# A streaming-encoder block in exact float32 products: narrow columns in the first value block's passes, norm weights on GpSimd's queue

## What is computed

```python
h = rms_norm(x, norm_gain)
proj = einsum('btd,de->bte', h, w_in)              # 9296 columns
qa, ka, va, ga, qb, kb, vb, gb, qi, ki, wi = split(proj)   # 8 x 1024, 1024, 64, 16
out_a = chunked_relpos_attention(qa, ka, va, rel_bias)
logits = einsum('bqhd,bsd->bqhs', qi, ki)
score = einsum('bqh,bqhs->bqs', wi * idx_scale, relu(logits))
sel = top_k(where(admissible, score, -inf), 64)
out_b = attention(qb, kb[sel], vb[sel], alibi)     # 8 heads of 128
y = concat(out_a * silu(ga), out_b * silu(gb))
out = rms_norm(x + y @ w_out, final_gain)
```

## Time and profile before

| | us |
|---|---|
| median of 3 runs | 530.44 (530.16 to 530.63) |
| the profiled execution's own time | 529.62 |
| its span from the first to the last instruction | 527.6 |

### The profile page before, as it was taken

One profiled execution on the slowest core, in us unless ns is written; L12 is line 12 of the kernel. 1 busy time (PEld: TensorE's weight loads), 2 busy tenths in 40 slices (PEclk: granted clock), 3 DMA queues, 4 the chain that ended last, 5 costly groups with the idle time before them and its releaser, 6 DMA issues.

```text
span 527.6 us, 8251 instructions
## 1 busy us (share of the span) xinstructions
PE 519.2 (98%) x2871; PEld 451.9 (86%) x2871; DVE 366.7 (70%) x551; ACT 273.8 (52%) x405; POOL 29.8 (6%) x46
## 2 busy tenths in 40 slices
PE   9999999999999999999999999999999999999994
PEld 6899998888888888888888888888888888888883
DVE  6898685665668766767676767586877887646454
ACT  6875544444543344445554637374655566434342
POOL 1005043150000000000000000000000000000000
PEclk9999999999999999999999999999999999999998
DMA  8966966658555555563746454645555775665614
GB/s 298 381 205 187 288 203 214 196 174 279 172 190 196 197 199 183 182 196 106 234 145 194 148 176 157 191 147 183 159 160 176 252 250 170 189 198 194 202 44 159
DMA packets 72668, 102.53 MB, mean 194 GB/s; under 512 B 3504, under 2 KB 61760, under 8 KB 72384
## 3 DMA queue, kind: packets, MB, share of 16 engines
q1 hardware_dynamic: 70944, 96.68, 56.7%
q0 software_dynamic: 1264, 5.00, 3.0%
q10 hardware_dynamic: 432, 0.47, 0.3%
HBM read 99.24 MB, written 2.11 MB: 192 GB/s over the span
## 4 chain that ended last, share of the span: by engine, by line
PE 98%; DVE 0%; ACT 0%; DVEq 0%; issue 0%
PE acc L426 38%; PE acc L424 18%; PE acc L391 11%; PE acc L392 11%; PE acc L393 11%; PE acc L429 1%; PE aux L496 1%; PE acc L457 1%; PE aux L585 1%; PE aux L606 1%; PE acc L439 1%; PE aux L611 0%; PE aux L583 0%; PE aux L612 0%; PE aux L613 0%; PE aux L527 0%
## 5 line engine op out<-in xcount | busy, mean ns | idle before, releaser
L426 PE MATMUL acc<-acts,w_hi 128*128 128x512 f32 (+1 forms) x896 | 304.8, 389 | 0.0
L960 DVE TENSOR_TENSOR w_lo<-w_raw,w_hi 128x1024 fp32r<-128x1024 f32 x172 | 213.2, 1244 | 107.3 <-ACT w_hi L674 106.0
L674 ACT ACTIVATE w_hi<-w_raw 128x1024 fp32r<-128x1024 f32 x172 | 181.7, 1058 | 156.8 <-PE acc L426 81.9
L424 PE MATMUL acc<-acts,w_lo 128*128 128x256 f32 (+1 forms) x840 | 232.8, 277 | 0.0
L426 PEld LDWEIGHTS acc<-acts,w_hi 128*128 128x128 f32 x896 | 166.5, 188 | 30.1
L424 PEld LDWEIGHTS acc<-acts,w_lo 128*128 128x128 f32 x840 | 158.6, 189 | 1.0
L391 PE MATMUL acc<-w_hi,acts 128*128 128x512 f32 x248 | 96.6, 389 | 0.0
L392 PE MATMUL acc<-w_lo,acts 128*128 128x512 f32 x248 | 96.5, 389 | 0.0
L393 PE MATMUL acc<-w_hi,acts 128*128 128x512 f32 x248 | 96.5, 389 | 0.0
L391 PEld LDWEIGHTS acc<-w_hi,acts 128*128 128x128 f32 x248 | 46.6, 188 | 10.0 <-issue 0.3
L392 PEld LDWEIGHTS acc<-w_lo,acts 128*128 128x128 f32 x248 | 46.6, 188 | 9.6
(11 more groups left out here) (179 smaller groups left out, 388.1 us busy)
## 6 DMA issues: line engine op xcount, KB each, us to landing
w_raw<-w_blocks SPq DMA_DIRECT2D x140, 512.0 KB, 3.6
w_raw<-wo_blocks SPq DMA_DIRECT2D x32, 512.0 KB, 4.3
w_raw<-w_blocks SPq DMA_DIRECT2D x8, 256.0 KB, 5.3
qk<-x POOLq DMA_DIRECT2D x1, 2048.0 KB, 10.7
qk<-xT SPq DMA_DIRECT2D x7, 256.0 KB, 6.0
o<-ext_dram POOLq DMA_DIRECT2D x1, 1024.0 KB, 8.1
fgain<-final_gain POOLq DMA_DIRECT2D x1, 1024.0 KB, 7.8
out<-o SPq DMA_DIRECT2D x2, 512.0 KB, 3.0
```

The costliest lines, as they stand in the source:

```text
L424: nc.tensor.matmul(acc[:, bank:bank + n], w_lo4[:, u % RING, q, c], a_hi[:, k, tokens], start=False, stop=False)
L426: last = nc.tensor.matmul(whole, w_hi4[:, u % RING, q, c], acts[:, k, :, tokens], start=(k == 0), stop=(k == KT - 1))
L674: nc.scalar.activation(flat(w_hi[:, s, :, :]), w_raw[:, s, :], ACT.Copy).then_inc(hi_done, 1)
L960: nc.vector.tensor_tensor(flat(w_lo[:, s, :, :]), w_raw[:, s, :], flat(w_hi[:, s, :, :]).bitcast(f32), ALU.subtract).then_inc(lo_done, 1)
```

## The change

The weights of block 0 get 80 more columns: every k of a slot is now 592 wide (512 of va and 80 narrow), and each of its passes is made as two of 296 columns, the first into the old bank of `acc`, the second into `aux[0]` or `aux[1]` (216 columns of va and the 80 narrow ones, with tokens on partitions). The narrow passes, the copies and the three transposes go. Each unit's narrow weights come by a DMA of their own (two pieces of 320 bytes for each partition). The first k is loaded and split in parts of 296 columns and the rest; its narrow piece is issued on ScalarE's queue in the gain's old place, and the gain is GpSimd's first instruction. The norm sums move from after unit 2 of block 1 to after unit 0, block 0's results are read in two pieces each, the narrow ones straight from `aux`, and the transposes of `ki_nat` move from after unit 7 to before unit 6. The diff, cut:

```diff
+WIDE = CB + NARROW
+PART = WIDE // 2
+V_REST = CB - PART
...
+        raw_slots = sb("raw_slots", [P, RING, UK * WIDE])
...
+            def load_narrow(u):
+                sp.dma_start(raw_slots[:, u % RING, :].rearrange("p (k c) -> p k c", k=UK)[:, :, CB:WIDE],
+                             w_narrow[:, u * UK * NARROW:(u + 1) * UK * NARROW].rearrange("p (k c) -> p k c", k=UK)
+                             ).then_inc(nw_landed[u % RING], 16)
+
             for u in range(HALVED):
-                sp.dma_start(w_raw[:, u, 0:CB], w_blocks[VA_FIRST, u, :, 0:CB]).then_inc(half_landed[u], 16)
                 if u == 0:
+                    sp.dma_start(raw_slots[:, 0, 0:PART], w_blocks[VA_FIRST, 0, :, 0:PART]).then_inc(first_landed, 16)
+                    sp.dma_start(raw_slots[:, 0, PART:CB], w_blocks[VA_FIRST, 0, :, PART:CB]).then_inc(half_landed[0], 16)
                     sp.dma_start(xT_land[:, 1, :], xT[:, 1, :]).then_inc(xT_landed[0], 16)
-                sp.dma_start(w_raw[:, u, CB:2 * CB], w_blocks[VA_FIRST, u, :, CB:2 * CB]).then_inc(w_landed[u], 16)
+                else:
+                    load_narrow(u)
+                    sp.dma_start(raw_slots[:, u, 0:CB], w_blocks[VA_FIRST, u, :, 0:CB]).then_inc(half_landed[u], 16)
+                sp.dma_start(raw_slots[:, u, WIDE:WIDE + CB], w_blocks[VA_FIRST, u, :, CB:2 * CB]
+                             ).then_inc(w_landed[u], 16)
...
-            sp.dma_start(nw_raw[:, :], w_narrow).then_inc(nw_landed, 16)
...
         def _(pool):
+            pool.dma_start(gain[:, :], norm_gain).then_inc(gain_landed, 16)
...
-            pool.wait_ge(narrow_done, 1)
             split_q(0)
...
+            def wide_pass(k, part, a, w, start=False, stop=False):
+
+                c = (k % UK) * WIDE + part * PART
                 for m in range(TM):
-                    nc.tensor.matmul(acc[:, m * CB:m * CB + CB], a[:, 0, m * P:m * P + P], w[:, 0, 0, :],
-                                     start=start, stop=False)
+                    dst = (acc[:, m * CB:m * CB + PART], aux[m][:, 0:PART])[part]
+                    last = nc.tensor.matmul(dst, a[:, k, m * P:m * P + P], w[:, (k // UK) % RING, c:c + PART],
+                                            start=start, stop=stop)
+                return last
 
             pe.wait_ge(a0_done, 1)
+            pe.wait_ge(first_hi, 1)
+            wide_pass(0, 0, a_hi, hi_slots, start=True)
             pe.wait_ge(half_hi, 1)
-            first_k(a_hi, w_hi, True)
+            wide_pass(0, 1, a_hi, hi_slots, start=True)
             pe.wait_ge(alo_done, 1)
-            first_k(a_lo, w_hi, False)
+            for part in range(2):
+                wide_pass(0, part, a_lo, hi_slots)
+            pe.wait_ge(first_lo, 1)
+            wide_pass(0, 0, a_hi, lo_slots)
             pe.wait_ge(half_lo, 1)
-            first_k(a_hi, w_lo, False)
...
+                    for n, (a, w) in enumerate(((a_hi, hi_slots), (a_hi, lo_slots), (a_lo, hi_slots))):
+                        for part in range(2):
+                            last = wide_pass(k, part, a, w, stop=(k == KT - 1 and n == 2))
                 last.then_inc(mm_done, 1)
...
-            for u in range(3):
-                feature_unit(1, u, 1, CHUNK)
+            feature_unit(1, 0, 1, CHUNK)
             pe.wait_ge(cleared, 3 + HEADS)
             pe.wait_ge(summed, UNITS)
             nc.tensor.matmul(aux[2][:, 0:T], ones_mat[:, :], x_sum[:, 0:T], start=True, stop=True)
...
-            feature_unit(1, 3, 1, CHUNK)
-
-            pe.wait_ge(nlo_done, 1)
-            for k in range(KT):
-                for n, (w, a) in enumerate(((nw_hi, a_hi), (nw_hi, a_lo), (nw_lo, a_hi))):
-                    last = nc.tensor.matmul(aux[0][0:NARROW, 0:T], w[:, k, :], a[:, k, :],
-                                            start=(k == 0 and n == 0), stop=(k == KT - 1 and n == 2))
-            last.then_inc(narrow_done, 1)
+            for u in range(1, 4):
+                feature_unit(1, u, 1, CHUNK)
             both_out(1)
...
             act.dma_start(xT_land[:, 0, :], xT[:, 0, :]).then_inc(xT0_landed, 16)
-            act.dma_start(gain[:, :], norm_gain).then_inc(gain_landed, 16)
+            act.dma_start(raw_slots[:, 0, :].rearrange("p (k c) -> p k c", k=UK)[:, :, CB:WIDE],
+                          w_narrow[:, 0:UK * NARROW].rearrange("p (k c) -> p k c", k=UK)).then_inc(nw_landed[0], 16)
...
             split_lo(0, 8)
-            for u in range(1, 4):
+            for u in range(1, 3):
                 add_square(u)
             split_lo(0, 9)
+            add_square(3)
             add_square(4)
-            add_square(5)
             split_lo(0, 10)
-            add_square(6)
-            split_lo(0, 11)
-            add_square(7)
+            for u in range(5, UNITS):
+                add_square(u)
             dve.wait_ge(summed, UNITS - 1)
             nc.vector.tensor_tensor(x_sum[:, 0:T], x_sum[:, 0:T], x_sum[:, T:2 * T], ALU.add).then_inc(summed, 1)
...
+            split_lo(0, 11)
             dve.wait_ge(ssq_made, 1)
...
+            nc.vector.tensor_scalar(v1_flat[:, V_COLUMNS[0]], acc[:, CB:CB + PART], rstd[:, 1:2], None,
+                                    ALU.mult).then_inc(acc_out[1], 1)
+            nc.vector.tensor_scalar(v1_flat[:, V_COLUMNS[1]], aux[1][:, 0:V_REST], rstd[:, 1:2], None, ALU.mult)
...
+            split_lo(0, 13)
+            dve.wait_ge(std_done, 2)
+            nc.vector.reciprocal(rk[:, :], rk[:, :]).then_inc(rk_made, 1)
```

More of the change, by code:

```diff
@@ L146, in hybrid_block @@
         xT_landed = [sem(f"xT_landed{c}") for c in range(UNITS)]
-        nw_landed = sem("nw_landed")
+        first_landed = sem("first_landed")
+        nw_landed = [sem(f"nw_landed{s}") for s in range(RING)]
         gain_landed = sem("gain_landed")
@@ L463, in _ @@
                 pe.wait_ge((half_hi, hi_done)[k % UK], k // UK + 1)
-                early_k(k, a_hi, w_hi)
+                for part in range(2):
+                    wide_pass(k, part, a_hi, hi_slots)
                 pe.wait_ge(alo_done, k + 1)
-                early_k(k, a_lo, w_hi)
+                for part in range(2):
+                    wide_pass(k, part, a_lo, hi_slots)
                 pe.wait_ge((half_lo, lo_done)[k % UK], k // UK + 1)
-                last = early_k(k, a_hi, w_lo)
+                for part in range(2):
+                    last = wide_pass(k, part, a_hi, lo_slots)
                 if k % UK == UK - 1:
                     last.then_inc(mm_done, 1)
-            for u in range(2, HALVED):
+            for u in range(2, UNITS):
+                if u >= HALVED:
+                    pe.wait_ge(alo_done, UK * u + UK)
+                    pe.wait_ge(lo_done, u + 1)
                 for kk in range(UK):
                     k = u * UK + kk
[L474 to L478, removed]
-                last.then_inc(mm_done, 1)
-            for u in range(HALVED, UNITS):
-                pe.wait_ge(alo_done, UK * u + UK)
-                unit(0, u)
-            for u in range(3):
-                feature_unit(1, u, 1, CHUNK)
+                    if u < HALVED:
+                        pe.wait_ge(alo_done, k + 1)
+                        pe.wait_ge((half_lo, lo_done)[kk], u + 1)
+                    for n, (a, w) in enumerate(((a_hi, hi_slots), (a_hi, lo_slots), (a_lo, hi_slots))):
+                        for part in range(2):
+                            last = wide_pass(k, part, a, w, stop=(k == KT - 1 and n == 2))
+                last.then_inc(mm_done, 1)
+            feature_unit(1, 0, 1, CHUNK)
             pe.wait_ge(cleared, 3 + HEADS)
@@ L502, in _ @@
             pe.wait_ge(patterned, 1)
[L503 to L511, removed]
+            pe.wait_ge(aux_read[1], 1)
             for m in range(TM):
@@ L514, in _ @@
             last.then_inc(kit_done, 1)
+            feature_unit(1, 6, 1, CHUNK)
+            feature_unit(1, 7, 1, CHUNK)
             def index_late(i, c):
@@ L715, in _ @@
                     a_part(k)
-                split_hi(0, u)
+                act.wait_ge(w_landed[u % RING], 32)
+                act.wait_ge(nw_landed[u % RING], 32)
+                act.wait_ge(mm_done, u - RING + 1)
+                nc.scalar.activation(hi_slots[:, u % RING, :], raw_slots[:, u % RING, :], ACT.Copy).then_inc(hi_done, 1)
             def square_x(u):
@@ L1066, in _ @@
                                            ALU.mult).then_inc(rated, 1)
-            dve.wait_ge(rated, 2)
+            dve.wait_ge(mm_done, UNITS)
+            nc.vector.tensor_scalar(v1_flat[:, V_COLUMNS[0]], acc[:, CB:CB + PART], rstd[:, 1:2], None,
+                                    ALU.mult).then_inc(acc_out[1], 1)
+            nc.vector.tensor_scalar(v1_flat[:, V_COLUMNS[1]], aux[1][:, 0:V_REST], rstd[:, 1:2], None, ALU.mult)
+            dve.wait_ge(v_hi_done, 1)
+            for part, (c, src) in enumerate(zip(V_COLUMNS, (acc[:, 0:PART], aux[0][:, 0:V_REST]))):
```

(24 more changed lines are left out.)

130 lines of the change are left out of this document (64 added, 66 removed).

## The result

The changed kernel takes **533.82 us** (median of 7 runs, 533.28 to 537.52) against 530.16 us for the kernel before on the same chip (7 runs, 529.82 to 530.63): a ratio of 1.008, 95% interval 1.0064 to 1.0096. By the medians it is slower by 3.7 us (4.2 by the ratio), where 1.8 us less was forecast, and 533.82 lies above the whole range.

The account below looks back on a forecast made before the run. TensorE, busy 98%, was taken as the bound. With the third k at 9.1 us, the query block starts at 31.6 instead of 33.42 us; 1.8 us off the 530.44 us median gives 528.6, range 527.8 to 530.3.

Parts of the forecast that it names:

- After it, equal pace: After the query block's start, or unit 4 of it, later passes were to run at the same pace as before.
- That fits by 0.2 us, the thinnest margin: Norm sums after query unit 0: TensorE there at 33.9 us, the squares' sum ready at 33.6 to 33.7.
- Rival (3): Norm sums or a split behind VectorE's reads come 0.7 us or more late: 529.3 to 530.2 us, 9%.
- The transfers of a unit are no bound: Block 0's loads, three a unit now: 848 KB per 3.2 us is 264 GB/s, against 371 reached.
- 133.9 ns a pass: Block 0's 192 passes of 296 columns, priced between the 256- and 512-column passes: 25.7 us in all.
- rival (1): Block 0's 296-column passes cost the short pass's price, 145 ns or more: 530.7 to 531.8 us, 11%.
- The start: First microseconds: gain lands 4.0 us after issue (bounds 3.2 to 5.9), first pass at 5.1, third k at 9.1 us.
- 320-byte pieces: Narrow weight loads, 160 KB in 512 pieces: 0.43 us by bytes, 1.4 at 1 KB's price each; 0.75 taken.
- rival (2): Each narrow-weight piece costs as much as 1 KB (529.3 us) or 2 KB (every unit waits, up to 530.8): 8%.
- narrow stretch and transposes out, 192 passes in: TensorE, block 0: 27.5 us of wide and narrow passes and transposes removed, 25.7 added, 1.8 us less.

Follow-up runs that it names:

- e1: The changed kernel with the pitch of the hi and lo weight slots raised from 4736 to 4864 bytes, a multiple of 256: 530.66 us, ratio 1.0014.
- e2: The kernel before with the pitch of the hi and lo weight slots raised from 4096 to 4224 bytes, nothing else changed: 533.47 us, ratio 1.0064.
- e3: The changed kernel with the norm sums on TensorE after unit 1 of the query block instead of unit 0: 531.81 us, ratio 1.0041.
- e4: The changed kernel with both the 4864-byte slot pitch and the norm sums after unit 1 of the query block: 528.73 us, ratio 0.9975.
- e7: The kernel before with only the gain's load moved, from ScalarE's queue to the first place on GpSimd's: 530.24 us, ratio 0.9995.
- e9: e4 with the gain back as second DMA of ScalarE's queue and the first narrow piece third behind it: 530.24 us, ratio 1.0005.
- e5: The kernel before with a weight slot pitch of 4160 bytes, slots 0, 64, 128 and 192 bytes past a multiple of 256: 535.52 us, ratio 1.0096.
- e6: The kernel before with the activations' buffer moved by 128 bytes and every later buffer by 256: 535.9 us, ratio 1.0105.
- e10: e4 with the activations of k = 1 loaded third on ScalarE's queue instead of third on SyncE's: 528.39 us, ratio 0.9966.

## Why the prediction was wrong, point by point

The forecast of the span's change was -1.8 us, the measurement is +4.2, a miss of 6.0 us in the profiled executions.

- **"After it, equal pace": the step that failed most, 3.3 us.** The prediction took every later pass at its old price and never looked at where its operands now lie. The change declares the ring by the wide unit, and every later block reads it at 4736 bytes a slot. e1 takes the drift away, e2 puts it into the old kernel: shown from both sides. No rival had it. Why a place costs time is not shown.
- **"That fits by 0.2 us, the thinnest margin": a wait of 1.8 us, and 2.0 us by e3.** Rival (3) was the right mechanism at 9%; its end at 530.2 us allows 1.6 us, too little. VectorE, against the earlier trace rows:

```profile
30.08 1.22 DVE L982 TENSOR_TENSOR lo_slots<-raw_slots,hi_slots 128x1024 fp32r<-128x1024 f32 x1
31.22 1.48 DVE L1069 TENSOR_TENSOR o<-o 128x512 f32<-128x512 f32 x2
32.62 1.22 DVE L982 TENSOR_TENSOR lo_slots<-raw_slots,hi_slots 128x1024 fp32r<-128x1024 f32 x1
33.75 2.28 DVE L1069 TENSOR_TENSOR o<-o 128x512 f32<-128x512 f32 x3
36.06 0.42 DVE L1081 TENSOR_TENSOR o<-o 128x256 f32<-128x256 f32 x1
```

  A split of 1.22, the last three adds of 2.28 and the last add of 0.42 are what the sum used (1.2, 2.28, 0.43). What it left out is the queue in front, the first two rows here: the sum began at the end of TensorE's unit 6 (28.4), with one split to come. But VectorE had the split and adds of the unit before it to do first, to 32.6 us, and all of it stood behind late units. The chain that ended last (start, length, what), and ScalarE at the last two units of wide weights:

```profile
16.33 7.45 DMA raw_slots<-w_blocks
...
24.90 1.14 ACT o L743 x3
...
26.46 1.06 ACT hi_slots L687
...
27.54 1.23 DVE lo_slots L982
```
```profile
21.51 1.19 ACT L741 ACTIVATE hi_slots<-raw_slots 128x1184 fp32r<-128x1184 f32 x1 [0.98 <-DMA raw_slots<-w_blocks]
...
23.80 1.20 ACT L741 ACTIVATE hi_slots<-raw_slots 128x1184 fp32r<-128x1184 f32 x1 [0.30 <-DMA raw_slots<-w_blocks]
```

  The last unit of wide weights, issued at 16.33 us when VectorE had freed its slot, is there at 23.78; ScalarE waits 0.98 us for the unit before it and 0.30 for this one. Its own order does the rest: the splits come first, then the squares, and only behind the squares does VectorE add. The chain needs 36.5 us where TensorE is ready at 34.84 (36.64 - 1.80). "The transfers of a unit are no bound" held for TensorE, which never waited for them, and not for this chain. In e4 VectorE's last add ends at 35.53 us and TensorE comes to the sums at 36.81: one unit's move is enough.
- **"133.9 ns a pass": 0.45 us.** It is 136.1 to 136.5; rival (1), 145 and more, did not come. 192 x 2.3 ns = 0.45 us. The sum also had the k follow one another without a gap; the three dear first passes add 0.2 us.
- **The start: right to 0.15 us in its end, and not in its parts.** The gain landed 3.4 us after its issue (4.0 taken, 3.2 to 5.9 the bounds), and GpSimd's row of the issue starts at 1.26 us, not at the 0.7 that I took from where its memsets used to start. The Trainium skill, "DMA: Bandwidth & Descriptors", section "Anatomy of one DMA — SWDGE (gpsimd) path", has about 2.0 us fixed for this path; this trace does not agree, with 3.4 us for 8 KB counted from the start of the issuing row, which itself lasts 0.68 us. The second k started at 7.38 (7.1 forecast), the third at 9.25 (9.1).
- **320-byte pieces: rival (2)'s prices did not come.** DMA issues of the changed kernel, 0 to 60 us:

```profile
qk<-xT ACTq DMA_DIRECT2D x1, 128.0 KB, 3.2
...
raw_slots<-w_narrow ACTq DMA_DIRECT2D x1, 80.0 KB, 3.3
gain<-norm_gain POOLq DMA_DIRECT2D x1, 8.0 KB, 3.4
```

  The same queue's other transfer takes as long, the third k came 0.15 us late, not 0.65, and TensorE never waits more than 0.1 us for a later unit. A smaller cost is there: with the DMA engines busy throughout, from 9 to 18 us, the changed kernel moves 381 to 389 GB/s and the kernel before 400 to 408, and the narrow pieces are what is new in the stream.
- **The saving was real.** 1.8 (wait at the sums) + 0.45 (pass price) + 0.2 (first passes) + 0.15 (start) + 3.3 (pitch) = 5.9 of the 6.0 us missed. With the two large ones mended, e4 is 1.3 us faster than the runs of the kernel before beside it, and 1.2 us in the profiled spans: the forecast 1.8 less the pass price and the start. So that part of the sum, narrow stretch and transposes out, 192 passes in, was sound. That e4's 528.73 us stands so near the forecast 528.6 is in part luck, as the forecast was counted from 530.44 us and the runs beside e4 have 530.01.

## What to carry to other kernels

When a buffer's unit changes size, list the byte offset of every slice that TensorE reads from it later, in code that the diff leaves alone, and keep the pitch a multiple of 256 bytes; here that was worth 3.3 us, more than the 1.8 that the change was to bring. When a consumer is moved earlier, follow its producer's *queue* of work back to the last thing that was late, not only the producer's own instructions from a tidy start. A saved transfer slot can be worth nothing in one kernel (e7) and 1.5 us in the next (e9), when something takes the slot.

## What the runs showed of the hardware

- **The place of a TensorE operand in SBUF has a price.** Per 512-column pass of this type, at the granted clock of 1.00: 226.7 ns with both operands on multiples of 256 bytes; with the streamed one off, in the second k of a slot, 228.9 at 64 bytes (e5), 233.1 to 233.4 at 128 (e2, e5, the changed kernel) and 233.3 at 192 (e5); 232.4 with the held one 128 off (e6). A feature pair of 512 and 256 columns takes 350.5 with both in place, 352.6 with the streamed operand off (e6), and with the held one off 351.6 to 351.7 (two slots of four at 128 bytes, the changed kernel and e2) and 353.3 (three of four, e5). The Trainium skill, "SBUF — State Buffer", section "Operand start alignment", asks for a multiple of the element size and says that its runs timed nothing. By it, places 64, 128 and 192 bytes off are legal for 4-byte elements; here they cost up to 3%.
- It isn't seen in passes of 296 columns: 136.0 ns in place, 135.7 at 128 bytes off. The first k of a slot that is itself in place, behind one that is off, takes 228.9 for 226.7; that too is unexplained.
- The first transfer of GpSimd's queue took 3.4 to 3.5 us for 8 KB in every kernel that had the gain there. The first of the kernel before took 5.2, but was issued at 19.1 us, amid the stream of weights. The third transfer of ScalarE's queue took 5.3 and 5.1 us (e9, e10), though 80 and 128 KB; the third of SyncE's, issued at the same time, 3.3 to 4.3.
